# Moving the surplus-token branch ahead of the last memory product, turning mixer 2's input between that product's halves, and reordering small steps at three places of mixer 1

## The reference

```python
def first_block(...):
    xn = rmsnorm(h, norm_mix); h = h + token_mixer(xn, ...)      # mixer 1: two kinds of attention
    hn = rmsnorm(h, norm_ffn); h = h + hierarchical_moe(hn, ...) # 32 experts, 2 per token
def second_block(x, mem, ...):
    hn = _rmsnorm(x, norm_mix); z = hn @ w_in                    # mixer 2: LRU and chunk attention
    ...
    x = x + y @ w_out
    x = x + _memory_cross_attention(_rmsnorm(x, norm_cross), _rmsnorm(mem, norm_mem), w_q, w_kv, w_o)
    x = x + _peer(_rmsnorm(x, norm_ffn), ...)                    # 16384 small experts
    return _rmsnorm(x, norm_final)
```

## Time and profile before

| | us |
|---|---|
| three runs: median (lowest to highest) | 1752.03 (1751.58 to 1756.85) |
| the profiled execution | 1753.53 |
| its span, first to last instruction | 1752.1 |

### The profile page before, as it was taken

The page is one execution under the profiler, slowest core; times in us unless marked ns, Lnnn a source line. Parts: engine busy times, 40 slices in busy tenths (PEclk is TensorE's granted clock), DMA queues, the critical chain, the costliest instruction groups (busy, mean ns, idle before and its releaser), DMA issues.

```text
span 1752.1 us, 23300 instructions
## 1 busy us (share of the span) xinstructions
PE 1628.7 (93%) x9505; PEld 1285.5 (73%) x9505; DVE 929.7 (53%) x1462; ACT 687.9 (39%) x1021; POOL 544.3 (31%) x323
## 2 busy tenths in 40 slices
PE   6889999999999998699989999999999879999997
PEld 5767874545454543588879999999999768888886
DVE  4664432111111111465545288788723798889896
ACT  5552421110110010456535344434344895454543
POOL 3110100000000000321213143443455897677670
PEclk8988999999999999798999999999999999999999
DMA  7432589999999999353525456556566308999994
GB/s 259 133 97 72 225 343 402 421 421 421 422 421 421 421 422 414 111 181 97 181 72 169 145 185 202 181 181 203 179 234 206 106 16 285 360 351 349 347 353 150
DMA packets 99343, 444.79 MB, mean 254 GB/s; under 512 B 11153, under 2 KB 19857, under 8 KB 57633
## 3 DMA queue, kind: packets, MB, share of 16 engines
q1 hardware_dynamic: 85696, 403.85, 61.5%
q0 software_dynamic: 11264, 33.60, 5.2%
q10 hardware_dynamic: 2272, 5.82, 0.9%
HBM read 435.26 MB, written 7.86 MB: 253 GB/s over the span
## 4 chain that ended last, share of the span: by engine, by line
PE 73%; DMA 11%; ACT 7%; DVE 5%; issue 3%; ACTq 0%; SPq 0%; DVEq 0%
PE ps L468 12%; PE ps L638 11%; PE ps L469 11%; PE ps L470 11%; PE ps L1074 10%; PE ps L1067 7%; DMA big<-in_w_up 5%; DMA fix<-in_w_up 5%; PE ps L661 2%; ACT y L2320 2%; DMA hl<-in_w_up 2%; PE ps L598 1%; PE ps L703 1%; PE ps L621 1%; DVE fix_parts L1105 1%
## 5 line engine op out<-in xcount | busy, mean ns | idle before, releaser
L2360 POOL TENSOR_TENSOR fix_parts<-fix,fix_parts 128x512 fp32r<-128x512 f32 x59 | 143.1, 2428 | 739.7 <-ACT fix_parts L1926 739.7
L470 PE MATMUL ps<-hh_parts,fix_parts 128*128 128x256 f32 x1120 | 318.4, 284 | 0.0
L1105 DVE TENSOR_TENSOR fix_parts<-fix,fix_parts 128x1536 fp32r<-128x1536 f32 (+1 forms) x84 | 169.8, 2021 | 116.8 <-ACT fix_parts L1926 111.5
L468 PE MATMUL ps<-hh_parts,fix_parts 128*128 128x256 f32 x768 | 219.3, 286 | 9.9 <-issue 5.8
L469 PE MATMUL ps<-hl_parts,fix_parts 128*128 128x256 f32 x768 | 217.8, 284 | 0.0
L470 PEld LDWEIGHTS ps<-hh_parts,fix_parts 128*128 128x128 f32 x1120 | 216.2, 193 | 0.0
L638 PE MATMUL ps<-big 128*64 128x512 f32 x784 | 197.9, 594 | 10.4 <-DMA big<-in_w_up 4.9
L1926 ACT ACTIVATE fix_parts<-fix 128x2048 fp32r<-128x2048 f32 x84 | 160.6, 1914 | 66.9 <-PE ps L1074 55.2
L638 PEld LDWEIGHTS ps<-big 128*64 128x64 f32 x784 | 68.9, 137 | 128.3 <-issue 127.4
L468 PEld LDWEIGHTS ps<-hh_parts,fix_parts 128*128 128x128 f32 x768 | 147.7, 192 | 11.6 <-issue 11.6
L638 PE MATMUL ps<-fix,big 128*64 128x512 f32 x528 | 143.5, 594 | 5.8 <-DMA fix<-in_w_up 3.5
(11 more groups left out here) (398 smaller groups left out, 3836.5 us busy)
## 6 DMA issues: line engine op xcount, KB each, us to landing
fix<-in_expert_u SPq DMA_DIRECT2D x64, 1024.0 KB
fix<-in_expert_v SPq DMA_DIRECT2D x38, 1024.0 KB
big<-in_w_up SPq DMA_DIRECT2D x35, 1024.0 KB, 22.1
big<-in_w_gate SPq DMA_DIRECT2D x33, 1024.0 KB, 19.4
big<-in_w_down SPq DMA_DIRECT2D x30, 1024.0 KB, 23.0
big<-in_expert_v SPq DMA_DIRECT2D x26, 1024.0 KB
fix<-in_w_gate SPq DMA_DIRECT2D x23, 1024.0 KB, 21.1
fix<-in_w_down SPq DMA_DIRECT2D x22, 1024.0 KB, 24.0
```

The costliest lines, as they stand in the source:

```text
L468: pe.matmul(o, l[0], r[0], start=first, stop=False)
L470: return pe.matmul(o, l[1], r[0], start=False, stop=last)
L1105: nc.vector.tensor_tensor(m.fr(x[:, 0:end]), x[:, 0:end], m.fr(hi[:, 0:end]).bitcast(F32), ALU.subtract).then_inc(s.lo_v, 1)
L2360: nc.gpsimd.tensor_tensor(m.fr(x[:, at:2048]), x[:, at:2048], m.fr(hi[:, at:2048]).bitcast(F32), ALU.subtract).then_inc(s.lo_g, 1)
```

## The change

- `BEATS1`: `memnorm` is split; DVE's part (`memroot`) goes with `qksq 3` to beat 7, `qkroot 1` and `rope 1` to beat 8, `qkscale 1` to beat 9, and ACT's scaling of the memory rows to beat 11. `group 0` and `qkscale 0` go from beat 22 to 23, behind `outdturn`; on DVE both beats come ahead of the tile's low half, on ACT ahead of the last two `leave` copies.
- The loads of the memory rows (2 x 512 KB) and gain rows (two of 128 pieces of 32 bytes) are issued by SP behind the fifth tile, not by ACT.
- The branch goes ahead of `vm1` on all engines. `vm1`'s first half follows it, then PE waits for `joined`, turns x, and does `vm1`'s second half. ACT takes `vm1` out of PSUM after turning x, and issues the two gate loads after that. DVE does the low half of `xlru`'s first tile behind the branch, and one more low half behind the diagonals.
- `rows` goes from mixer 2's beat 0 to beat 2: after 72 of `xlru`'s 96 matmuls, not 24.

```diff
 BEATS1 = {
-    1: [("narrow", 0)], 4: [("qksq", 2)], 5: [("memsum", 0), ("rope", 0)], 7: [("memnorm", 0)],
-    8: [("qksq", 3)], 9: [("qkroot", 1), ("rope", 1)], 10: [("qkscale", 1)], 12: [("qkturn", 1)],
+    1: [("narrow", 0)], 4: [("qksq", 2)], 5: [("memsum", 0), ("rope", 0)], 7: [("qksq", 3), ("memroot", 0)],
+    8: [("qkroot", 1), ("rope", 1)], 9: [("qkscale", 1)], 11: [("memnorm", 0)], 12: [("qkturn", 1)],
...
-    22: [("memturn", 0), ("group", 0), ("qkscale", 0)], 23: [("outdturn", 0)], 24: [("qkturn", 0)],
+    22: [("memturn", 0)], 23: [("outdturn", 0), ("group", 0), ("qkscale", 0)], 24: [("qkturn", 0)],
...
 BEATS2 = {
-    0: [("rows", 0)], 4: [("conv", 0)], 5: [("conv", 1)], 6: [("conv", 2)], 7: [("gates", 0)], 8: [("gates", 1)],
+    2: [("rows", 0)], 4: [("conv", 0)], 5: [("conv", 1)], 6: [("conv", 2)], 7: [("gates", 0)], 8: [("gates", 1)],
@@ tensor_first
     pe_scatter(pe, m, s, 15, range(4))
-    pe_product(pe, m, s, t, "vm1", f["w_vm1"], 4, before, m.MT, "mem", rank, None)
@@ tensor_second
-    pe.wait_ge(s.joined, 1)
-    pe_turn(pe, m, s, m.X, "mix2")
+    for h in range(2):
+        if h:
+            pe.wait_ge(s.joined, 1)
+            pe_turn(pe, m, s, m.X, "mix2")
+        for b in range(2):
+            pe_tokens(pe, m, s, t, f["w_vm1"] + h, h, b, 4 + b, before["vm1"][4 + b], m.MT, "mem")
@@ vector_first
-            elif what == "memnorm":
+            elif what == "memroot":
                 dve_rstd(nc, s, v, "mem", m.mss)
...
     def tile_beats(tile, at):
         beat(at)
+        if at == 22:
+            beat(at + 1)
         low(t.split[tile] + AHEAD)
-        beat(at + 1)
+        if at != 22:
+            beat(at + 1)
@@ dve_experts
-    dve_low(nc, m, s, t, t.n_first + 2)
     v.settle()
@@ vector_second
     ve.tensor_scalar(m.ss[:, 2:4], m.iota[:, 0:2], 1.0, None, ALU.mult).then_inc(s.joined, 1)
+    dve_low(nc, m, s, t, t.n_first + 2)
     dve_turn(nc, m, s, "mix2", m.g_mix2, m.HT[1], m.HT[0])
     dve_low(nc, m, s, t, t.n_first + 3)
-    dve_low(nc, m, s, t, t.n_first + 4)
...
     diag("mix2", m.DG)
+    dve_low(nc, m, s, t, t.n_first + 4)
@@ scalar_first
     act_turn(nc, m, s, "mix", m.g_mix, m.HT[0])
-    for b in range(2):
-        ac.dma_start(m.MEM[:, b, :], a["mem_2"][0, b * P:(b + 1) * P, :]).then_inc(s.mem_in, 16)
-    for i, c0 in enumerate((8, 56)):
-        ac.dma_start(m.GROWS[8 * i:8 * i + 8, :].rearrange("k (a b) -> k a b", a=16),
-                     a["pack"][:, c0:c0 + 8].rearrange("(k a) b -> k a b", a=16)).then_inc(s.gains_in, 16)
...
+        if i == 5:
+            beat(4 * i + 3)
         for b in range(2):
             leave(tile, 4 + 2 * (i % 2), m.PROJ[:, b, 512 * x:512 * x + 512], b, rs[:, b:b + 1])
-        beat(4 * i + 3)
+        if i < 5:
+            beat(4 * i + 3)
...
-    for b in range(2):
-        leave(f["w_vm1"], 4, m.VM[:, b, 512:1024], b)
     ac.wait_ge(s.flag, 1)
@@ scalar_second
     ac.wait_ge(s.joined, 1)
+    act_turn(nc, m, s, "mix2", m.g_mix2, m.HT[0])
+    act_high(nc, m, s, t, t.n_first + 3)
+    for b in range(2):
+        ac.wait_ge(s.used, t.used[f["w_vm1"] + 1] - 1 + b)
+        ac.activation(m.VM[:, b, 512:1024], m.PS[:, 4 + b, :], ACT.Copy).then_inc(s.out_a, 1)
     ac.dma_start(m.GW[:, 0], a["gate_a_w_2"]).then_inc(s.lru_in, 16)
     ac.dma_start(m.GW[:, 1], a["gate_x_w_2"]).then_inc(s.lru_in, 16)
-    act_turn(nc, m, s, "mix2", m.g_mix2, m.HT[0])
-    act_high(nc, m, s, t, t.n_first + 3)
     act_sums(nc, m, s, o, "mix2", m.X, m.SQ2, m.ss)
@@ sync_first
-    for i in range(2, t.cut):
+    for i in range(2, 5):
+        sync_tile(nc, m, s, t, i)
+    for b in range(2):
+        sy.dma_start(m.MEM[:, b, :], a["mem_2"][0, b * P:(b + 1) * P, :]).then_inc(s.mem_in, 16)
+    for i, c0 in enumerate((8, 56)):
+        sy.dma_start(m.GROWS[8 * i:8 * i + 8, :].rearrange("k (a b) -> k a b", a=16),
+                     a["pack"][:, c0:c0 + 8].rearrange("(k a) b -> k a b", a=16)).then_inc(s.gains_in, 16)
+    for i in range(5, t.cut):
         sync_tile(nc, m, s, t, i)
```

More of the change, by code:

```diff
@@ L2527, in body_tensor @@
                 ins.then_inc(s.ov_t, 1)
+        pe.wait_ge(s.ov_v, per_v * 32 + 1)
     def body_scalar():
```

## The result

The changed kernel takes 1728.83 us (median of six runs, 1722.13 to 1732.25) where the kernel before takes 1752.60 (six runs beside them, 1751.58 to 1756.90): a ratio of 0.9855, 95% interval 0.9833 to 0.9877. That is 23.8 us gained. The profiled execution took 1729.55, its span 1728.2, for 1753.53 and 1752.1 before. The forecast was 1722; the sign and the range held, the gain was forecast 6.7 us too large.

A forecast was written before the change was run, and what follows sets the result against it. It took PE's waits for late work of other engines, at four places, as what bounds the kernel. 2.0 + 7.3 + 5.0 + 16.2 = 30.5 us off 1753.53 gave 1723.0, the median 1.5 lower, say 1722; range 1715 to 1737.

The forecast's parts named there:

- (a): At the branch: PE's gap is 5.3 us with the low clock level behind it, total gain 25, 1727 us; chance 0.13.
- (b): At the start: gain rows come late, turning +2.0 us into -3.8, total gain 24.7, 1728 us; chance 0.07.
- (d): In mixer 2's first product: diagonals miss the third quarter, PE drops to the low level, 5 us lost, 1727; chance 0.10.
- Part 1: At the start: moving memory and gain-row loads off ACT's queue lets PE's first product start 2.0 us earlier.
- Part 2: At the first queries and keys: the reordered work cuts PE's 5.33 us stall and the low clock behind it, 7.3 us.
- Part 3: At the memory turning and first output half: output halves go ahead of group sum and scaling, gaining 5.0 us.
- (c): In the expert layer: its stream does not start earlier, so gains ahead of it are lost, 1736 us; chance 0.09.
- The clock term: Behind removed stalls: PE's work at the low clock level costs nearly double; 1.6 and 1.0 us counted at first queries and keys.
- Part 4: At the branch between the blocks: 4.7 us at the product's start, 12.0 in the product, less 0.5, gaining 16.2 us.
- the sum's best bound: At the start of mixer 2's first product: with a branch gap of 1.38 us the gain was put at 5.1 us.
- The cover that was named the narrowest of the sum: In mixer 2's first product: the diagonals are ready at 728.7, 0.9 us before the row needs them at 729.6.
- (e): In the expert layer: its stream slips against PE, up to 125 us more, 1847 us; chance 0.04 with anything like it.

The follow-up runs named there:

- part 1 undone: The changed kernel with the memory and gain rows loaded from ScalarE's queue again: 1728.83 us, ratio 0.9863 to the kernel before.
- part 2 undone: The changed kernel with squares, roots and rope of the first heads ordered as before: 1732.88 us, ratio 0.9887 to the kernel before.

## Why the prediction was right, and where its size was off

- **In the range, outside the forecast's own band.** 1728.83 lies within 1715 to 1737, but not in 1717 to 1726, which had the chance of 0.52; it lies in 1726 to 1732, which rivals (a), (b) and (d) held with 0.30 together. Of these only (a)'s gap came. The largest piece of the miss, in the attention, had neither a term nor a rival, and that width kept for other causes covered it is luck.
- **Part 1, forecast 2.0: the step was right, the gain did not last.** The first product moved 17.81 to 15.87, 1.94. The bound that was feared, gain rows late by 5.8, did not come: SP issued them by 16.8 and PE did not wait ahead of its small transpose (26.77), so their place behind the memory rows cost nothing here. But in the one trace with part 1 undone the first expert product comes no later than with it, and the medians (0.0 to 0.2 us apart) can't tell 0 from 2. As far as the traces show, its 2 us are given back at the low level before the experts begin. "After each of them PE is fed by PE-paced work, so I carry a shift there to the end" is the sentence that failed here.
- **Part 2, forecast 7.3: right at its place.** With part 2 undone the next stalled step (the transposes at 82.29 in the changed kernel) comes at 89.64, 7.35 later. The wait is gone rather than 0.5, the 16 transposes take 1.94. At the first expert product 5.3 to 7.2 of it are left. The two places, changed kernel first:

```profile
82.29 2.00 PE L621 MATMUL ps<-big 128*128 128x64 f32 x16 [1.49 <-DVE big L1211]
```
```profile
89.64 2.62 PE L621 MATMUL ps<-big 128*128 128x64 f32 x16 [1.50 <-DVE big L1211]
```

- **Part 3, forecast 5.0: right at its place.** PE starts 1.0 behind DVE's first output half (115.83, DVE at 114.82), as taken, and the wait falls by 4.55 for a forecast of 4.6. From the eight transposes to the first score it is 17.44 before and 12.70 after, 4.7 less, small waits of 0.74 and 1.02 included; over all traces 17.1 to 17.9 in five without part 3, 12.6 to 12.7 in nine with it. At the first expert product 0.9 to 2.8 are left.
- **Parts 1 to 3 together, 14.3 forecast up to the scores: 15.4 found** in the first pair of traces, 13.7 to 17.4 between any of the three before and the three after; up to the experts 10.8, and 8.6 to 11.4. Rival (c), that the experts' stream absorbs them, did not happen: the expert stretch lasts 468.70 for 467.87, and lies between 467.9 and 469.9 in all fourteen traces, so that the 0.8 is no effect of the change.
- **The clock term was mis-sized.** The prediction let the low level change only right behind the stalls that it removed, always for the better. The attention, where PE hardly waits at all, has 17.1 us of it before and 27.3 after; 10.2 / 2 = 5.1 us is the largest piece of the miss. No rival held it.
- **Part 4, the gap: forecast 2.5, measured 5.01.** The prediction chose a value near DVE's 2.12 and kept ACT's 5.3 as the upper end and as rival (a). Rival (a) was right on the gap, and its low level came too, for about 1.5. 2.12 and 1.38 in the trace of before were not the branch's price but what queued work left uncovered: DVE's is 3.51 with only its additions to x ahead. The gap is no fixed length behind the scatter either. From the scatter's start to `vm1`'s first matmul it is 7.1 to 7.2 us in seven of the eight traces with the branch there (6.5 in the eighth), with gaps of 5.0 to 5.1 where the scatter took 2.1 and of 3.0 to 3.8 where it took 3.5; the forecast had 3.5 + 2.5 = 6.0, so 1.1 was missing there. (By its own terms the sum's best bound, a gap of 1.38, is 5.8 and not 5.1 at the product's start.) The rule of the Trainium skill that was weighed there ("Runtime: NRT & Kernel Launch", section on instruction fetch mechanics: a taken branch to a page not at hand stalls until it is fetched) agrees with the rows as far as they go, with 3.3 on PE and 3.5 on DVE; no run here shows the fetch itself.
- **The product's start, forecast 4.7 ahead of the scatter's shift: 2.3.** From the scatter's start, 18.9 was forecast and 21.25 came: 2.5 more for the gap, 1.5 more for the low level, 1.4 less because the scatter itself ran at the high level (2.11 us for 3.48), 0.3 less for the turning (706.09 to its next matmul at 707.76).
- **The product, forecast 24.1 to 12.1: 12.4 (713.33 to 725.72).** The cover that was named the narrowest of the sum, 0.9 us, was 2.9: the diagonals were ready at 719.0, and the row's turn came at 721.96. Rival (d) did not happen. What made it wider is in the last section: the prediction took 2.5 us for the reciprocal and the two diagonals, and they took 0.7 (718.35 to 719.03).
- **The sum.** 15.4 up to the scores, less 4.6 in the attention, less 0.8 in the experts, plus 13.8, is 23.8. The slower rival (e) had no trace: the waits for the experts' tiles are 5.5 us in six, for 6.1 in six.

## What to carry to other kernels

A gap that the profile shows at a branch is what the queued work did not cover, not what the branch costs: read its price off the engine with the least queued ahead of it, or plan with that as the value and not as the bound. Count it from the start of the work ahead, and subtract two gaps only where that work took equally long. Where a stall is taken out of a kernel that PE bounds, look up the granted clock of the next stretch too, and keep a share of the gain back for it: here 4.6 of 15.4 us were gone within the next 100 us, in work that was not touched. And check a wait's label against when the named work ended; 3.5 us between the two here meant another cause.

## What the runs showed of the hardware

- **The low clock level without standing.** From 140 to 180 of the span PE is busy for all of the 40 us in both kernels, and the granted clock is 0.83 before and 0.76 after (stretches of before, then of after; by the time of the span, so the work in them is some 15 us apart):

```profile
140.00:180.00 40.00, 40.00 (x196) 29.89 (x194) 15.05 (x23) 12.41 (x34) 4.10 (x2) 0.83 0.24 80
```
```profile
140.00:180.00 40.00, 40.00 (x210) 33.91 (x210) 14.41 (x26) 14.22 (x37) 4.14 (x4) 0.76 0.20 63
```

  The Trainium skill, "TensorE: Matmul & The Clock Gate", Part 1, tells that the clock is released by activity and falls with idleness. Behind the stalls the traces agree: in the kernel before the clock was low from 64.1 to 70.9, around the end of the wait of 5.33, and a low piece stands there in all five traces that have this wait and in none of the nine that haven't. (The first 60 us tell less: 0.91, 0.91 and 0.94 in three traces of before, 1.00, 0.94 and 0.94 in three of after.) In the attention PE hardly waits in any of them and the clock is lower where stalls ahead were removed; there the measurement decides, and its cause is open.
- **DVE's small steps beside GpSimd.** In the kernel before, the two diagonal steps had GpSimd's subtractions running over them:

```profile
735.90 1.09 DVE L1580 TENSOR_SCALAR y<-ii,small 128x128 f32<-128x128 f32 x1
...
734.07 2.83 POOL L2360 TENSOR_TENSOR big_parts<-big,fix_parts 128x512 fp32r<-128x512 f32 x1 [2.64 <-ACT fix_parts L1926]
736.87 1.26 POOL L2360 TENSOR_TENSOR fix_parts<-fix,fix_parts 128x512 fp32r<-128x512 f32 x1
```

  The second took 1.30 and ended at 738.21, just behind GpSimd's second subtraction (738.13). After, they took 0.29 and 0.28 (the second is at 718.75 above), with GpSimd at rest from 714.6 to 720.2. So it is in all fourteen traces: 1.09 and 1.30 in the four with the old order, 0.28 to 0.29 in the ten with the new. The Trainium skill, "SBUF — State Buffer", section on the two separate sides, says that these two engines share one pair of ports that an instruction holds for its whole length, where DVE's instruction is of a form that uses it; the rows agree. The change kept them apart by putting a tile's low half behind the diagonals instead of ahead (that low half waits for the same high half of ACT that starts GpSimd), and that is where most of the 2 us of extra cover came from.
- **The branch, with little queued ahead of it,** costs 3.3 us on PE (beyond a wait of 1.7 that stood there anyway) and 3.5 on DVE, flag load included, on a path that enters no body. With the 48 matmuls of `vm1` ahead of it, 1.3 to 1.6 us of standing stayed on PE (four traces).
